# Attention in a two-block transformer kernel: transpose-mode turns, values as queries x channels, 64-row score products

## The chip, the cores and the metric

The kernel runs on one core of a Trainium2 chip. Its time is the device time of one execution in microseconds (us): the median of three runs. One more execution was taken by the hardware profiler, and everything read from the trace belongs to that one.

## The reference

Two layers of a latent transformer with context tokens and then one block of another design are computed in float32, on 512 latent tokens, 256 context tokens and a width of 1024. The change touches the three attentions alone. Cut to what matters:

```python
def dense_gqa_blocks(q, k, v):                # layer 0: 8 heads, 2 key heads, 768 keys
    s = jnp.einsum('bqkgd,btkd->bkgqt', qblk, k) * scale
    p = jax.nn.softmax(s, axis=-1).astype(v.dtype)
    return jnp.einsum('bkgqt,btkd->bqkgd', p, v)

def window_gqa_blocks(q, k, v, k_ctx, v_ctx, sink):   # layer 1: 16 heads, |q-k| <= 128, plus 256 context keys
    p = jax.nn.softmax(jnp.concatenate([s_w, s_c, s_s], axis=-1), axis=-1)   # s_s: one sink logit per head
    o = jnp.einsum('bkgqt,btkd->bqkgd', p[..., :BAND_LEN], vblk)
    o = o + jnp.einsum('bkgqt,btkd->bqkgd', p[..., BAND_LEN:BAND_LEN + C], v_ctx)

def chunked_attention(q, k, v, rel_bias):      # second block: 8 heads, chunks of 64, a relative bias
    scores = jnp.einsum('bnqhd,bnkhd->bhnqk', q, kb) * (ATT_HEAD_DIM ** -0.5) + bias
    p = jax.nn.softmax(jnp.where(valid, scores, min), axis=-1)
    out = jnp.einsum('bhnqk,bnkhd->bnqhd', p, vb)
```

In layer 0 the context queries attend to the context keys too.

## The kernel before

Channels lie on the partitions and tokens along the rows of a tile. Every large product is made in three passes of reduced float32: each operand is held as a high part and a low part, and high x high, high x low and low x high are summed in PSUM. Weight blocks of 128 x 1024 flow through a ring of four: SyncE loads them (`load_block`), ScalarE makes the high part (`split_hi`, L265), GpSimd the low part (`split_lo`, L271), TensorE uses them (`product`, L294). The engines run five programs written by hand; the order of the work is the order of the code, and semaphores hold them together.

The three attentions (`l0_att`, `l1_att`, `s_att`) use one set of functions, `att_pe`, `att_act`, `att_dve` and `att_pool`. The work is cut in units: one head and one tile of 128 queries. `ATT_ITERS` is 4, and one iteration has 12 units in l0, 16 in l1, 8 in s, so there are 48, 64 and 32 units. A unit has as many key blocks of 128 as its queries see: 6 in l0 (2 for context queries), 4 or 5 in l1, 1 to 4 in s; over all units that is 592 blocks. In l0 and l1 the two middle iterations are a loop on the engines (`Fori`), in s they are written out.

What TensorE does for a unit:

- `qk` (L1241): scores, queries x keys. A chunk of q holds two heads of 64 channels. GpSimd first copies the queries with the other head's 64 rows set to zero (`att_stage`, L1407), so that the product runs over 128 rows. In l1 the window mask is added by products with an identity (L1244), in s the relative bias.
- `turn` (L1258): for each block, `prob` (the exponentials, queries x keys) is the weight and `dg` the moving operand. `dg` is a diagonal with one over the row sum, so the product is the transposed and already divided probability, keys x queries, in ordinary float32.
- `values` (L1271): for each block three products, with v (128 keys x 64 channels) as the weight and the turned probabilities `pt_hi`, `pt_lo` (128 keys x 128 queries) moving. The result is 64 channels x 128 queries.

TensorE's order within unit u is `qk(u+2)`, `turn(u)`, `values(u-1)`. VectorE finds the row maximum (L1355, or L1358 and L1360 where there is a sink), makes the reciprocal and `dg` (L1377, L1379) and the low part `pt_lo` (L1366). ScalarE makes the exponentials with their row sum (L1301, and the sink's exponential, L1304), the high part `pt_hi` (L1331) and copies the result into `opair` (L1314), of which it makes the high part (L1319) and GpSimd the low part (L1426). `prob`, `pt_hi`, `pt_lo` and the score banks have two buffers each. In l0, VectorE also does twelve reductions over 128 x 1024 for the modulation vectors (`mod_block`, L339), six in the first iteration and six in the last.

## Time and profile before

| | us |
|---|---|
| median of 3 runs | 3029.43 |
| lowest, highest | 3028.75, 3034.0 |
| the profiled execution | 3029.36 |
| its span | 3027.6 |
| TensorE busy in it | 2899.5 |
| VectorE, ScalarE, GpSimd busy | 1686.7, 1050.2, 1145.4 |

The span is from the first instruction to the last; 1.8 us of the profiled execution's time lie around it. Busy is the union of an engine's instructions; since matmuls are pipelined and overlap in the record, the time from one start to the next is the price of one, and not its duration. A PE row with 128*128 has a weight of 128 rows x 128 columns; 128x64 or 128x512 after it is what moves through. An ordinary float32 product has two records for one instruction of the program.

### The profile page before, as it was taken

To read this page: it belongs to the slowest core of one execution; us is meant where nothing else is said; L and a number is where in the kernel's file an instruction comes from. 1 tells how busy PE (TensorE), PEld (TensorE's weight loads), DVE (VectorE), ACT (ScalarE), POOL (GpSimd) and SP (SyncE) were. 2 spreads that over 40 slices of the span, in tenths; PEclk is the share of its full clock that TensorE was granted. 3 is DMA by queue.
4 is the path that set the end of the run, shared out by engine and by line. 5 is a ranking of instruction groups with operands and counts; after the bars stand their busy time and mean duration, and the time that the engine had idled before them with its cause. 6 is when DMAs were issued, how large, how long until landed. Compare 5 with 4: busy or idle time off the path is not lost.

```text
span 3027.6 us, 43720 instructions
## 1 busy us (share of the span) xinstructions
PE 2899.5 (96%) x15898; PEld 2441.1 (81%) x15898; DVE 1686.7 (56%) x2794; ACT 1050.2 (35%) x1926; POOL 1145.4 (38%) x782
## 2 busy tenths in 40 slices
PE   8889999999999979999999999999999979899998
PEld 6779878888888769987888878888788758688886
DVE  5577886555545667775555564444544674432223
ACT  3247332111111437753222242222354673222222
POOL 1333223333333153323554544544353324334443
PEclk8989999999999999999999999999999999999999
DMA  5100333323232020032444423443202212122221
GB/s 217 53 28 8 120 111 135 115 89 113 88 119 90 28 78 2 1 118 92 146 169 171 145 91 139 145 152 132 101 26 81 81 61 99 68 84 97 97 97 56
DMA packets 78454, 290.91 MB, mean 96 GB/s; under 512 B 8833, under 2 KB 8961, under 8 KB 76929
## 3 DMA queue, kind: packets, MB, share of 16 engines
q1 hardware_dynamic: 78338, 289.36, 26.8%
q8 instruction: 73, 1.20, 0.2%
q14 instruction: 43, 0.35, 0.0%
HBM read 287.23 MB, written 2.10 MB: 96 GB/s over the span
## 4 chain that ended last, share of the span: by engine, by line
PE 85%; DVE 10%; ACT 3%; issue 1%; POOL 1%; DMA 0%; ACTq 0%; DVEq 0%; SPq 0%; POOLq 0%
PE ps L294 68%; PE ps L1258 4%; PE ps L1241 4%; PE ps L1271 3%; PE ps L494 2%; PE ps L350 1%; DVE ps L601 1%; PE ps L1516 1%; PE ps L1244 1%; DVE xl L608 1%; DVE rec L1711 1%; PE ps L955 1%; DVE r_g L1703 1%; DVE qn L1084 1%; PE ps L947 1%
## 5 line engine op out<-in xcount | busy, mean ns | idle before, releaser
L271 POOL TENSOR_TENSOR w_lo<-raw,w_hi 128x1024 fp32r<-128x1024 f32 x367 | 929.2, 2540 | 1445.4 <-ACT w_hi L265 1445.4
L265 ACT ACTIVATE w_hi<-raw 128x1024 fp32r<-128x1024 f32 x367 | 384.1, 1057 | 1355.0 <-PE ps L294 1251.1
L294 PE MATMUL ps<-n_hi,w_hi 128*128 128x512 f32 x1504 | 594.5, 395 | 12.4 <-DVE n_lo L1742 4.9
L294 PE MATMUL ps<-n_hi,w_lo 128*128 128x512 f32 x1504 | 587.4, 391 | 0.0
L294 PE MATMUL ps<-n_lo,w_hi 128*128 128x512 f32 x1504 | 587.4, 391 | 0.0
L820 DVE TENSOR_TENSOR y<-y,ps 128x512 f32<-128x512 f32 (+1 forms) x440 | 270.9, 633 | 266.1 <-PE ps L294 266.0
L339 DVE CUSTOM_DVE_ANT_0 dump<-modraw 128x1024 f32<-128x1024 f32 x212 | 356.9, 1683 | 13.8 <-DMA modraw<-mod_stream 7.9
L294 PEld LDWEIGHTS ps<-n_hi,w_hi 128*128 128x128 f32 x1504 | 283.7, 189 | 81.3 <-issue 11.7
L775 DVE TENSOR_TENSOR ps<-ffn_silu,ps 128x512 f32<-128x512 f32 x110 | 68.5, 641 | 481.0 <-PE ps L294 464.8
L294 PEld LDWEIGHTS ps<-n_lo,w_hi 128*128 128x128 f32 x1504 | 283.8, 189 | 60.6 <-issue 2.9
L294 PEld LDWEIGHTS ps<-n_hi,w_lo 128*128 128x128 f32 x1504 | 283.5, 189 | 59.3
L294 PE MATMUL ps<-h_hi,w_hi 128*128 128x512 f32 (+1 forms) x1072 | 291.8, 348 | 22.0 <-DVE h_lo L569 8.1
L294 PE MATMUL ps<-ffn_hi,w_hi 128*128 128x512 f32 x880 | 299.2, 372 | 1.3 <-DVE ffn_lo L782 0.8
L294 PE MATMUL ps<-ffn_lo,w_hi 128*128 128x512 f32 x880 | 297.7, 371 | 0.0
L294 PE MATMUL ps<-ffn_hi,w_lo 128*128 128x512 f32 x880 | 295.9, 369 | 0.0
L294 PE MATMUL ps<-h_lo,w_hi 128*128 128x512 f32 (+1 forms) x1072 | 293.4, 349 | 0.0
L294 PE MATMUL ps<-h_hi,w_lo 128*128 128x512 f32 (+1 forms) x1072 | 289.0, 345 | 0.0
L294 PEld LDWEIGHTS ps<-h_hi,w_hi 128*128 128x128 f32 x1072 | 169.7, 191 | 50.7 <-issue 20.3
L294 PEld LDWEIGHTS ps<-h_hi,w_lo 128*128 128x128 f32 x1072 | 171.1, 192 | 28.2
L294 PEld LDWEIGHTS ps<-h_lo,w_hi 128*128 128x128 f32 x1072 | 170.1, 192 | 24.3
L294 PEld LDWEIGHTS ps<-ffn_hi,w_hi 128*128 128x128 f32 x880 | 152.6, 188 | 33.3 <-DVE y L820 2.0
L294 PEld LDWEIGHTS ps<-ffn_hi,w_lo 128*128 128x128 f32 x880 | 153.6, 188 | 29.5
(292 smaller groups left out, 4287.1 us busy)
## 6 DMA issues: line engine op xcount, KB each, us to landing
raw<-w_stream SPq DMA_DIRECT2D x367, 512.0 KB, 3.4
modraw<-mod_stream SPq DMA_DIRECT2D x152, 512.0 KB, 3.2
mod_pair<-mod_first SPq DMA_DIRECT2D x7, 1024.0 KB, 12.5
xl<-x_in SPq DMA_DIRECT2D x1, 2048.0 KB, 7.6
out<-xl SPq DMA_DIRECT2D x8, 256.0 KB, 2.0
xc<-ctx_in SPq DMA_DIRECT2D x1, 1024.0 KB, 9.7
modraw<-mod_first SPq DMA_DIRECT2D x1, 1024.0 KB, 14.9
rel<-rel_in SPq DMA_DIRECT2D x1, 1024.0 KB, 4.7
```

What stands on the lines that cost most here:

```text
L265: nc.scalar.activation(w_hi[:, c % RING, :], raw[:, c % RING, :], ACT.Copy).then_inc(hi_ready, 1)
L271: nc.gpsimd.tensor_tensor(w_lo[:, c % RING, :], raw[:, c % RING, :], w_hi[:, c % RING, :].bitcast(F32), ALU.subtract).then_inc(lo_ready, 1)
L294: mm = nc.tensor.matmul(out, w[a], x[b][:, off:off + n], start=first and i == 0, stop=last and i == 2)
L339: nc.vector.tensor_tensor_reduce(where, modraw[:, slot, :], c_rows[:, m, :] if c < MOD2 else c2_row, 1.0, 0.0, ALU.mult, ALU.add, outs[m]) ...
L350: mm = nc.tensor.matmul(ps[:, 3, 2 * k:2 * k + 2], mod_pairs[k][:, 0, j * P:(j + 1) * P], c_cols[:, j, :], start=j == 0, stop=j == KC - 1)
L494: mm = nc.tensor.matmul(ps[:, sum_bank(name, si), 0:n], ones[:, :], square_buffer(name, k)[0][:, off:off + n], start=k == 0, stop=k == KC - 1)
L601: ins = nc.vector.scalar_tensor_tensor(out=product_chunk(name, k, si) if k in DVE_ADDS else t, in0=t, scalar=vec_g[:, slot, k, si:si + 1], ...
L775: nc.vector.tensor_tensor(up_bank(m % 2, si), f["silu"][:, m % 2, off:off + n], up_bank(m % 2, si), ALU.mult).then_inc(sem(f["name"] + "_h ...
L820: ins = nc.vector.tensor_tensor(acc, acc, out_bank(f, n, si, last), ALU.add)
L1241: mm = nc.tensor.matmul(score(u, col, w), (qs_hi, qs_lo)[x][:, qt % 2, half, :], a["k"][z][:, kc, kcol:kcol + w], start=i == 0, stop=i == ...
L1258: mm = nc.tensor.matmul(ps[:, 4 + g, (b - b0) * P:(b - b0 + 1) * P], prob[:, u % 2, b * P:(b + 1) * P], dg[:, u % 2, :], start=True, stop= ...
L1271: mm = nc.tensor.matmul(ps[0:HD, 6 + u % 2, 0:P], a["v"][z][:, x[4][b], a["vcol"](c, x)], (pt_hi, pt_lo)[p][:, u % 2, b * P:(b + 1) * P], ...
```

## The change

- `turn` becomes TensorE's transpose mode: the weight is `prob` as before, the moving operand is the identity. `dg` is gone.
- `values` swaps its operands: `pt_hi` and `pt_lo` (128 queries wide) are the weight and v (64 channels) moves. The result is 128 queries x 64 channels; ScalarE multiplies it by the reciprocal of the row sum while it copies it into `opair`.
- Since `opair` is now queries x channels, each pair of heads is turned once more (`pair_turn`), and the high and low parts of that are made by ScalarE and VectorE from PSUM.
- `qk` takes the 64 rows of the head straight from q and k. The staging on GpSimd is gone.
- In l1 the sink's logit is written as one more column of the scores, by an ordinary float32 product of `ones` with a 128 x 1 column. Row maximum, exponential and sum take it in; the separate steps for it are gone.
- The twelve modulation reductions in l0 go to GpSimd, which multiplies and then adds halves ten times (`mod_block_pool`).
- The loops over the iterations are written out on all engines.

```diff
-    opair, dg = at("opair", [2, P], SCR + 10240), at("dg", [2, P], SCR + 11264)
-    dump_att = at("dump_att", [BLK], SCR + 6144)
+    opair, mod_prod = at("opair", [2, P], SCR + 10240), at("mod_prod", [BLK], SCR + 6144)
...
+    def mod_block_pool(pool, c, outs):
+
+        ops, each = mods_of(c)
+        slot, turn = (c - MOD_FIRST) % MOD_RING, (c - MOD_FIRST) // MOD_RING
+        pool.wait_ge(mod_landed[slot], 16 * (turn + 1))
+        for m in range(each):
+            pool.wait_ge(mod_ops, ops + m)
+            nc.gpsimd.tensor_tensor(mod_prod[:], modraw[:, slot, :], c_rows[:, m, :], ALU.mult).then_inc(mod_halves, 1)
+            for j in range(HALVINGS):
+                pool.wait_ge(mod_halves, (ops + m - 2 * KC) * HALVINGS + j + 1)
+                n = BLK >> (j + 1)
+                last = j == HALVINGS - 1
+                nc.gpsimd.tensor_tensor(outs[m] if last else mod_prod[:, 0:n], mod_prod[:, 0:n], mod_prod[:, n:2 * n], ALU.add
+                                        ).then_inc(mod_ops if last else mod_halves, 1)
...
             for col, kcol, w in keys:
                 added = [m for m in more if col <= m[0] < col + w]
-                for i, (x, z) in enumerate(((0, 0), (0, 1), (1, 0))):
-                    mm = nc.tensor.matmul(score(u, col, w), (qs_hi, qs_lo)[x][:, qt % 2, half, :],
-                                          a["k"][z][:, kc, kcol:kcol + w], start=i == 0, stop=i == 2 and not added)
+                for j, (y, z) in enumerate(((0, 0), (0, 1), (1, 0))):
+                    mm = nc.tensor.matmul(score(i, col, w), a["q"][y][rows, qc, q0:q0 + P], a["k"][z][rows, kc, kcol:kcol + w],
+                                          start=j == 0, stop=j == 2 and not added)
...
+            if a["sink"]:
+                n = a["sink"](c, x)
+                mm = nc.tensor.matmul(score(i, score_width(a, i) - 1, 1), ones[:, :], sinks[:, n:n + 1], start=True, stop=True)
...
+        def pair_turn(p):
+            pe.wait_ge(a["s_o"], 2 * p + 2)
+            nc.tensor.transpose(PAIR_OUT, opair[:, p % 2, :], ident).then_inc(a["s_ot"], 1)
+
+        def turn(i):
+
+            pe.wait_ge(a["s_p"], i + 1)
+            for g, (b0, b1) in enumerate(a["groups"][i]):
+                if i > 0:
+                    pe.wait_ge(a["s_lo"], a["cum"][i - 1] + min(g + 1, len(a["groups"][i - 1])))
+                if g == 0 and pair_beside(i - 1) is not None:
+                    pe.wait_ge(a["s_m_lo"], pair_beside(i - 1) + 1)
+                if g == 0 and pair_beside(i) is not None:
+                    pair_turn(pair_beside(i))
                 for b in range(b0, b1):
-                    mm = nc.tensor.matmul(ps[:, 4 + g, (b - b0) * P:(b - b0 + 1) * P], prob[:, u % 2, b * P:(b + 1) * P],
-                                          dg[:, u % 2, :], start=True, stop=True)
+                    mm = nc.tensor.transpose(ps[:, 4 + g, (b - b0) * P:(b - b0 + 1) * P], prob[:, i % 2, b * P:(b + 1) * P], ident)
                 mm.then_inc(a["s_t"], 1)
...
                 for b in range(b0, b1):
-                    for i, (z, p) in enumerate(((0, 0), (0, 1), (1, 0))):
-                        mm = nc.tensor.matmul(ps[0:HD, 6 + u % 2, 0:P], a["v"][z][:, x[4][b], a["vcol"](c, x)],
-                                              (pt_hi, pt_lo)[p][:, u % 2, b * P:(b + 1) * P], start=b == 0 and i == 0,
-                                              stop=b == nb - 1 and i == 2)
+                    for j, (p, z) in enumerate(((0, 0), (0, 1), (1, 0))):
+                        mm = nc.tensor.matmul(head_out(i), (pt_hi, pt_lo)[p][:, i % 2, b * P:(b + 1) * P],
+                                              a["v"][z][:, blocks[b], a["vcol"](c, x)], start=b == 0 and j == 0,
+                                              stop=b == len(blocks) - 1 and j == 2)
             mm.then_inc(a["s_pv"], 1)
...
+        def out(i):
+
+            p, half = i // 2, i % 2
+            act.wait_ge(a["s_pv"], i + 1)
+            act.wait_ge(a["s_rinv"], i + 1)
+            if half == 0 and p >= 2:
+                act.wait_ge(a["s_ot"], p - 1)
+            nc.scalar.activation(opair[:, p % 2, half * HD:(half + 1) * HD], head_out(i), ACT.Copy,
+                                 scale=rinv[:, i % 4:i % 4 + 1]).then_inc(a["s_o"], 1)
+
+        def mixed_hi(p):
+            c, x = a["units"][2 * p]
+            act.wait_ge(a["s_ot"], p + 1)
+            nc.scalar.activation(a["out"][0][:, a["outchunk"](c, x), x[2]:x[2] + P], PAIR_OUT, ACT.Copy
+                                 ).then_inc(a["s_m_hi"], 1)
...
-        att_dve(dve, l0_att, att_mods)
+        att_dve(dve, l0_att)
...
-        att_pool_first(pool, l0_att, lambda eng: eng.wait_ge(l0_in["lo"], 5))
         split_lo(pool, FIRST["l0_pool"] + RING)
-        att_pool(pool, l0_att)
+        for c in range(MOD_FIRST, MOD_IN):
+            mod_block_pool(pool, c, [modv_a[m][:, c:c + 1] for m in range(2)])
```

The order of the instructions on TensorE in the fourth unit of l0, from its last score product on, before. In a row the moving operand stands first after the arrow and the weight second; `l_k` and `l_v` are keys and values, and the shape is that of the output.

```order
L1241 MATMUL ps<-l_k_hi,qs_lo 128x256
L1258 MATMUL ps<-dg,prob 128x128 [waits l0_att_lo,l0_att_diag]
L1258 MATMUL ps<-dg,prob 128x128 x2
L1258 MATMUL ps<-dg,prob 128x128 [waits l0_att_lo]
L1258 MATMUL ps<-dg,prob 128x128 x2
L1271 MATMUL ps<-pt_hi,l_v_hi 64x128 [waits l0_att_lo,l0_att_o]
L1271 MATMUL ps<-pt_lo,l_v_hi 64x128
L1271 MATMUL ps<-pt_hi,l_v_lo 64x128
```

The same place now; `loaded` is the tile that holds the identity.

```order
L1244 MATMUL ps<-l_k_hi,l_q_lo 128x256
L1255 MATMUL ps<-loaded,opair 128x128 [waits l0_att_o,l0_att_lo,l0_att_p]
L1268 MATMUL ps<-loaded,prob 128x128 x3
L1268 MATMUL ps<-loaded,prob 128x128 [waits l0_att_lo]
L1268 MATMUL ps<-loaded,prob 128x128 x2
L1280 MATMUL ps<-l_v_hi,pt_hi 128x64 [waits l0_att_lo,l0_att_o]
L1280 MATMUL ps<-l_v_lo,pt_hi 128x64
L1280 MATMUL ps<-l_v_hi,pt_lo 128x64
```

The number of instructions for a block stays at one turn and three value products. One turn for a pair of heads has come in, with its wait for ScalarE's copies, and `pt_hi` and `pt_lo` now stand second, as weights, where `l_v` stood.

On GpSimd, between the last weight split of l0's input stage and its first attention work, there stood the staging of queries:

```order
L271 TENSOR_TENSOR w_lo<-raw,w_hi 128x1024 [waits hi_ready] x3
L1407 TENSOR_TENSOR qs_hi<-l_q_hi,loaded 128x128 [waits lo_ready,l0_in_lo]
L1407 TENSOR_TENSOR qs_hi<-l_q_hi,loaded 128x128
L1407 TENSOR_TENSOR qs_lo<-l_q_lo,loaded 128x128 x2
L1407 TENSOR_TENSOR qs_hi<-l_q_hi,loaded 128x128 x2
L1407 TENSOR_TENSOR qs_lo<-l_q_lo,loaded 128x128 x2
```

In its place stand the modulation reductions, twelve times a product and ten halvings:

```order
L270 TENSOR_TENSOR w_lo<-raw,w_hi 128x1024 [waits hi_ready] x4
L349 TENSOR_TENSOR mod_prod<-modraw 128x1024 [waits mod_ops,mod_landed0]
L354 TENSOR_TENSOR mod_prod<-mod_prod 128x512 [waits mod_halves]
L354 TENSOR_TENSOR mod_prod<-mod_prod 128x256 [waits mod_halves]
L354 TENSOR_TENSOR mod_prod<-mod_prod 128x128 [waits mod_halves]
L354 TENSOR_TENSOR mod_prod<-mod_prod 128x64 [waits mod_halves]
L354 TENSOR_TENSOR mod_prod<-mod_prod 128x32 [waits mod_halves]
```

What TensorE's first score product waited for on GpSimd is no longer there; GpSimd reads instead what SyncE loads into `modraw`.

## Rows read from the trace of the kernel before

**Rows 1.** The page: its first line, the engines' busy time, TensorE's clock.
```profile
PE 2899.5 (96%) x15898; PEld 2441.1 (81%) x15898; DVE 1686.7 (56%) x2794; ACT 1050.2 (35%) x1926; POOL 1145.4 (38%) x782
...
PEclk8989999999999999999999999999999999999999
```

**Rows 2.** Busy time by stretch, middle of each attention: stretch, length, engines, PEclk, DMA.
```profile
204.00:330.00 126.00, 121.82 (x1258) 116.86 (x1256) 101.60 (x242) 85.36 (x240) 41.91 (x102) 1.00 0.06 22
...
1150.00:1322.00 172.00, 172.00 (x1862) 171.91 (x1861) 136.16 (x415) 123.04 (x387) 53.93 (x142) 1.00 0.01 1
...
2250.00:2296.00 46.00, 45.15 (x417) 42.99 (x414) 33.14 (x108) 33.63 (x124) 18.41 (x48) 1.00 0.01 2
```

**Rows 3.** L1271 alone in the whole of each attention: PE, PEld, PEclk, DMA.
```profile
190.00:334.00 144.00, 52.30 (x672) 46.83 (x672) 0.97 0.07 23
1136.00:1327.00 191.00, 67.33 (x864) 59.95 (x864) 0.99 0.01 1
2227.00:2296.00 69.00, 22.06 (x240) 18.41 (x240) 0.98 0.00 1
```

**Rows 4.** Groups by line and shape, TensorE: count, busy us, mean ns, idle before.
```profile
L1258 PE MATMUL ps<-dg,prob 128*128 128x128 f32 x1184 | 160.7, 279 | 5.0 <-DVE pt_lo L1366 4.8
```

**Rows 5.** Timeline of one six-block unit in l0, TensorE: start, us, engine, line.
```profile
241.03 0.45 PE L1241 MATMUL ps<-l_k_hi,qs_hi 128*128 128x512 f32 x1
...
242.13 1.50 PE L1258 MATMUL ps<-dg,prob 128*128 128x128 f32 x12
243.38 0.30 PE L1271 MATMUL ps<-pt_hi,l_v_hi 128*64 128x128 f32 x1
243.53 0.22 PE L1271 MATMUL ps<-pt_lo,l_v_hi 128*64 128x128 f32 x1
243.58 0.22 PE L1271 MATMUL ps<-pt_hi,l_v_lo 128*64 128x128 f32 x1
...
244.54 0.45 PE L1241 MATMUL ps<-l_k_hi,qs_hi 128*128 128x512 f32 x1
```

**Rows 6.** Timeline, first and last of 34 products in l0's input stage.
```profile
87.79 0.28 PE L947 MATMUL ps<-w_hi,h_lo 128*128 128x128 f32 x1
...
91.47 0.27 PE L947 MATMUL ps<-w_hi,h_lo 128*128 128x128 f32 x1
```

**Rows 7.** Timeline of the first modulation products, two moving columns each.
```profile
26.96 1.95 PE L350 MATMUL ps<-c_cols,mod_pair 128*128 128x2 f32 x16 [1.08 <-DVE n_rstd L539]
28.77 1.93 PE L350 MATMUL ps<-c_cols,modraw 128*128 128x2 f32 x16
30.55 19.79 PE L350 MATMUL ps<-c_cols,mod_pair 128*128 128x2 f32 x94
```

**Rows 8.** Busy time by stretch, as rows 2, around those products and around L947.
```profile
20.00:30.00 10.00, 8.92 (x47) 5.94 (x45) 5.38 (x8) 6.60 (x11) 1.70 (x1) 1.00 1.02 424
30.00:40.00 10.00, 10.00 (x54) 10.00 (x53) 9.61 (x11) 0.00 (x0) 3.94 (x2) 0.55 1.01 413
40.00:50.00 10.00, 10.00 (x49) 10.00 (x49) 8.71 (x16) 0.00 (x0) 0.00 (x0) 0.50 0.04 16
80.00:90.00 10.00, 10.00 (x92) 10.00 (x91) 4.91 (x4) 1.46 (x3) 4.12 (x2) 1.00 0.17 54
```

**Rows 9.** TensorE's waits in l0's attention: us in total, times, longest.
```profile
PE ps L1258 <- DVE pt_lo L1366: 4.4, 6, 2.1
```

**Rows 10.** Timeline of the start of l1's attention.
```profile
1131.81 0.22 DVE L2006 CAST ident_r<-loaded 128x128 fp32r<-128x128 f32 x1
...
1136.11 0.83 DVE L1086 TENSOR_TENSOR l_q_lo<-qraw,l_q_hi 128x512 fp32r<-128x512 f32 x1 [0.70 <-ACT l_q_hi L983]
...
1136.53 0.55 PE L1241 MATMUL ps<-l_k_hi,qs_hi 128*128 128x256 f32 x1 [16.57 <-POOL qs_lo L1407]
...
1138.37 0.69 DVE L1358 TENSOR_REDUCE smax<-ps 128x1 f32<-128x512 f32 x1 [1.44 <-PE ps L1244]
```

**Rows 11.** Timeline, GpSimd beside l0's attention and l1's input stage.
```profile
191.56 2.38 POOL L271 TENSOR_TENSOR w_lo<-raw,w_hi 128x1024 fp32r<-128x1024 f32 x1 [11.98 <-ACT w_hi L265]
...
243.57 0.76 POOL L1407 TENSOR_TENSOR qs_lo<-l_q_lo,loaded 128x128 fp32r<-128x128 f32 x2
...
1118.77 1.79 POOL L1126 TENSOR_TENSOR tsh<-tsh,loaded 128x512 f32<-128x512 f32 x1 [2.81 <-DVE tsh L1080]
```

More of the change, by code:

```diff
@@ L81 @@
           ("edges", [4, 2, 8]),
-          ("nsink", [16]),
+          ("sinks", [16]),
           ("relc", [8]),
@@ L1176, in pool_dve, with attention @@
             ins.then_inc(st["mix_lo"], 1)
-    def attention(name, units, q, k, v, out, qchunk, kchunk, vcol, outchunk, next_block, extra=None, sink=None,
-                  unroll=False):
+    def attention(name, units, q, k, v, out, qchunk, kchunk, vcol, outchunk, next_block, ready, extra=None, sink=None):
+        whole = [(c, x) for c in range(ATT_ITERS) for x in units]
         groups = []
-        for x in units:
+        for _, x in whole:
             nb = len(x[4])
@@ L1193, in attention @@
             cum.append(cum[-1] + len(g))
-        return dict(name=name, units=units, q=q, k=k, v=v, out=out, qchunk=qchunk, kchunk=kchunk,
-                    vcol=vcol, outchunk=outchunk, extra=extra, sink=sink, groups=groups, cum=cum, nu=len(units), next=next_block, unroll=unroll, d_steps=3 if sink else 2,
+        return dict(name=name, units=whole, q=q, k=k, v=v, out=out, qchunk=qchunk, kchunk=kchunk, vcol=vcol,
+                    outchunk=outchunk, ready=ready, extra=extra, sink=sink, groups=groups, cum=cum, n=len(whole), next=next_block,
@@ new lines, in score_width, with turned, head_out, pair_beside @@
+    def score_width(a, i):
+        return P * len(a["units"][i][1][4]) + (1 if a["sink"] else 0)
+    def turned(g, b0, b1):
+        return ps[:, 4 + g, 0:(b1 - b0) * P]
+    def head_out(i):
+        return ps[:, 6 + i % 2, 0:HD]
+    PAIR_OUT = ps[:, 4, 3 * P:4 * P]
+    def pair_beside(i):
+        return (i - 3) // 2 if i >= 3 and i % 2 else None
+    def att_pe(pe, a, free):
+        def qk(i):
+            c, x = a["units"][i]
+            _, half, q0, keys, _, _ = x
+            a["ready"](pe, c, x)
+            rows = slice(half * HD, (half + 1) * HD)
+            qc, kc = a["qchunk"](c, x), a["kchunk"](c, x)
+            more = a["extra"](c, x) if a["extra"] else []
@@ L1274, in values @@
             mm.then_inc(a["s_pv"], 1)
-        def body(c, first, last):
-            for u in range(nu):
-                n = ahead(a, c, u, last)
-                if n:
-                    qk_next(c, u, n)
-                turn(c, u, first)
-                n = behind(a, c, u, first, 1, nu)
-                if n:
-                    values(*n, first)
-            if last:
-                values(c, nu - 1, False)
-        free(pe)
-        qk(0, 0)
-        qk(0, 1)
-        att_loop(pe, a, body)
@@ L1411, in att_pool_first @@
-    def att_pool_first(pool, a, ready):
-        ready(pool)
-        pool.wait_ge(lo_ready, a["next"] + (RING - 1 - a["next"]) % RING + 1)
-        for qt in range(2):
-            att_stage(pool, a, 0, qt, True)
-    def att_pool(pool, a):
-        nt = a["nu"] // 2
-        def m_lo(c, p):
-            pool.wait_ge(a["s_m_hi"], c * nt + p + 1)
-            x = a["units"][2 * p]
+        free(pe)
+        qk(0)
+        qk(1)
+        for i in range(a["n"]):
+            if i + 2 < a["n"]:
+                pe.wait_ge(a["s_p"], i + 1)
+                qk(i + 2)
+            turn(i)
+            if i >= 1:
+                values(i - 1)
@@ L1425, in m_lo @@
             n = a["outchunk"](c, x)
[L1426 removed]
+            dve.wait_ge(a["s_m_hi"], p + 1)
+            nc.vector.tensor_tensor(a["out"][1][:, n, x[2]:x[2] + P], PAIR_OUT,
                                     a["out"][0][:, n, x[2]:x[2] + P].bitcast(F32), ALU.subtract).then_inc(a["s_m_lo"], 1)
[L1429 to L1438 removed]
@@ L1440, in att_pool @@
-        att_loop(pool, a, body)
+        row_max(0)
+        row_max(1)
+        inverse(0)
+        for i in range(a["n"]):
+            if i + 1 < a["n"]:
+                inverse(i + 1)
+            if i + 2 < a["n"]:
+                row_max(i + 2)
+            for g in range(len(a["groups"][i])):
+                low(i, g)
+                if g == 0 and pair_beside(i) is not None:
+                    mixed_lo(pair_beside(i))
+        mixed_lo(a["n"] // 2 - 1)
     def m_done(eng, a):
-        eng.wait_ge(a["s_m_lo"], ATT_ITERS * a["nu"] // 2)
+        eng.wait_ge(a["s_m_lo"], a["n"] // 2)
```

247 lines of the change are left out of this document (66 added, 181 removed).

## The prediction

> **What bounds the kernel now.** I read the page first, then the busy time by stretch, then the timeline of one unit. TensorE is busy for 96% of the span, at nearly full clock [rows 1]. In the middle of the attentions it is busy for 121.8 of 126, 172.0 of 172 and 45.2 of 46 us, while VectorE has at most 81% and ScalarE at most 73% [rows 2]. So what the change does to TensorE's stream counts one for one, and what it takes off the other engines counts only where TensorE waited for them: in l0 4.4 us for `pt_lo` [rows 9] and one wait of 16.6 us at the head of l1's attention [rows 10]. The attentions take 144, 191 and 69 us with their edges [rows 3], 404 of the span. That is the field of the change.
>
> The timeline of a six-block unit of l0 gives the prices [rows 5]. It repeats after 244.54 - 241.03 = 3.51 us: scores 1.10 (241.03 to 242.13), turns 1.25 for 12 records (0.104 each, so 0.208 a block), values 1.16 for 18 products. Within the values, the first step of a unit is 0.15 and the others 0.06: 243.53 to 243.58 and on to the next.
>
> **Values.** 672 + 864 + 240 = 1776 products [rows 3]. Their weight had 64 columns and 128 moved; now the weight has 128 columns and 64 move. What does such a product cost? The nearest row is L947: the same kind of number, weight of 128 columns, 128 moving. It goes at (91.47 - 87.79) / 33 = 0.112 us [rows 6], nearly twice the 0.060 of the values, though as many columns move: the difference is the weight's width. And L350, where only two columns move, still takes 1.81 / 16 = 0.113 [rows 7]. So with a weight of 128 columns the load sets the pace, whether 2 or 128 columns move, and 64 lies between them. I take 0.112. The change is 1776 x 0.052 = +92.4 us. From below, 0.030 would be half of 0.060, if only moving columns counted: 1776 x -0.030 = -53 us. I keep that end for a rival.
>
> **Turns.** 1184 records in two for each of 592 blocks [rows 4]. The weight keeps 128 columns. If transpose mode takes one pass, the floor from rows 6 and 7 is 0.112 a block against 0.208: 592 x -0.096 = -56.8 us. If it stays at two records of 0.104, the gain is nothing. I take one pass, since an identity times data needs no product of parts, and keep 0 as the other end.
>
> **Turns of pairs and sinks.** Half the units make a pair turn: (48 + 64 + 32) / 2 = 72 x 0.112 = +8.1. The sink is one ordinary float32 product per unit of l1, two records, each with a weight of 128 columns and one column moving, as L350 has two: 64 x 2 x 0.112 = +14.3.
>
> **Score products of 64 rows.** The number of products and of moving columns stays, so I cost them as before where the load of the next weight is still hidden behind the running product. There is no row with 64 of 128 rows in this trace. What is new is that 64-row and 128-row products alternate: in l0 and s twice and in l1 two to four times a unit, 48 x 2 + 64 x 3 + 32 x 2 = 352 changes. The nearest row is the change from `turn` to `values`, whose first step is 0.15 and not 0.06, so about 0.08 more [rows 5]. 352 x 0.08 = 28 us at most, 0 at least; I take the middle, +14. The upper bound of another kind, that no weight load is hidden in them, is priced below.
>
> **The Trainium skill against these rows.** The Trainium skill, "TensorE: Matmul & The Clock Gate", section "Back-to-back issue gap", gives about 81 ns for each pair of weight load and product at 128 moving columns, which would mean that a load of 128 columns is partly hidden. By that figure, as an estimate, values would cost +37 us, turns -75, pair turns and sinks +16, and with the other terms the sum would be about -10 us, the other sign. The 33 steps at 0.112 here do not agree with it, and here the measurement decides.
>
> **Waits.** In l1 the 16.6 us look like a gift, and are not. The first score product now waits only for the mask and identity, ready at 1132.0, so it can start 4.5 us earlier. But the next in line is VectorE: it is busy with the last chunk of q until 1136.9 and starts its row maximum at 1138.4 [rows 10]. Nothing behind it moves by more than 1.5 us: -1.5. In l0 the modulation work leaves VectorE, and the `pt_lo` waits of 4.4 us go, since VectorE was idle for a fifth of that stretch even with that work in it [rows 2]: -4.4. Against this, each attention now ends with copy, pair turn, high part and low part, one step more than before: about 0.7 us three times, +2. In units of one and two blocks TensorE's share of a unit is short, and the longer chain turn, pair's high part, `pt_hi`, `pt_lo`, next turn may show: +2. Behind the new waits for `s_o` and `s_m_lo` TensorE's whole stream is queued, and in a unit of four blocks or more about 2 us of value products stand between them and their source, which hides them. Together -2.
>
> GpSimd's twelve reductions: 2.4 us for the product of 128 x 1024, at most 1.8 for 512, 0.4 at 128 (two in 0.76) [rows 11], so about 0.9 for 256, and six smaller ones at no more than 0.38. That is at most 7.8 each and 94 in all, from about 194 us on, done at about 288 where the next weight split is due after 334. They are hidden. If they weren't, the weight stream of l0's output stage would wait.
>
> **The sum.** 92.4 - 56.8 + 8.1 + 14.3 + 14 - 2 = +70 us. The profiled execution took 3029.36, 0.07 below the median of the runs, so the same number serves for both: 3029.4 + 70 = 3099 us. With 0 to 28 for the changes of height and a few us either way for the waits, this case has a range of its own of 3080 to 3120.
>
> **Rivals.**
> A. The clock falls. During L350 TensorE has a product in flight all the time, and the granted clock still goes from 1.00 to 0.55 and 0.50, that is from 2.4 to 1.2 GHz, soon after those products with two moving columns began; each then takes 0.21 (19.79 / 94) [rows 7, 8]. In the changed unit far fewer columns move: 3 x 768 for the scores, 768 for the turns, 18 x 64 for the values, 4224, where 7680 moved before in a similar time. Against it: at L947, with 128 columns moving in 0.112 us, the clock stayed at 1.00 [rows 8], and 4224 columns in about 3.9 us are the same share. The new attention has about 404 + 70 = 474 us. At the low level for a quarter of it, the cost is 118 more, 3218; for all of it, 3570. It decides from some 20 us of low clock. 13%, of which 10 beyond my range.
> The Trainium skill, the same page, section "Part 4: PE-mode transpose", says that transposes in this mode do not count as TensorE activity for the full clock. No row here shows it; it speaks for this rival and would take 768 of the 4224 columns away.
> B. The load of the weight doesn't bind in the values, and columns moved set the price. Then values cost nothing more at 0.060, and the sum is 70 - 92 = -22: 3007 us. At 0.030 it would be 2954. Anything between 0.030 and 0.072 is this rival. Rows 6 and 7 speak against it, at two different widths. It decides as soon as a value product costs less than 0.072 (70 / 1776 below 0.112). The Trainium skill's 81 ns of the section above, "Back-to-back issue gap" of "TensorE: Matmul & The Clock Gate", with the turns at that price too, would end at 3020, on this side; its chance is counted here. 7%, all faster.
> C. In 64-row products the next weight isn't loaded beside the running product. 240 + 480 + 96 = 816 score products (three for each run of keys in 144 units) would pay up to 0.112 more: +91, 3190 us. For it: the trace has no such product. Against it: 128-row ones hide the load fully. 9%.
> D. Transpose mode does not do what its name says here, and a turn costs its 0.208: +57, 3156 us. 10%.
> E. The terms cancel to within 6 us of before. 3%.
> The forecast has 58%.
>
> **How the numbers follow.** What a measurement of this kernel can tell from no change is about 0.2%, 6 us. Faster is B, 7%; the same is E, 3%; slower is the rest, 90%. The range reaches from 3070, ten below the own range since some price may lie between the bounds, to 3195, so that C and D are in it. Left out are B, E and most of A, 20%.
>
> **What would show it.** Right: in the changed profile the value products start 0.11 us apart, the turns have 592 + 72 records 0.11 apart, a six-block unit of l0 takes 3.8 to 4.0 us, TensorE is still without gaps in the middle of the attentions, the first score product of l1 starts near 1132 plus what l0 has lost and the turns behind it hardly earlier than before. Wrong: value products 0.06 or less apart (B), score products with gaps of 0.1 between them (C), 1184 turn records (D), a clock of 0.5 inside an attention (A), or GpSimd late with l0's output weights.

## The result and the profile after

The changed kernel takes **3492.1 us** (median of four runs, 3481.0 to 3493.9) against 3029.1 for the kernel before beside it: ratio 1.152, 95% interval 1.149 to 1.155. The forecast was 3099, with a range up to 3195. Rival A, the falling clock, is what happened, over the whole of the three attentions.

The first lines of the page after, which answer to [rows 1]:

```profile
span 3479.2 us, 41669 instructions
...
PE 3357.9 (97%) x15506; PEld 2845.1 (82%) x15506; DVE 1630.7 (47%) x2569; ACT 1033.9 (30%) x1862; POOL 1084.8 (31%) x554
...
PEclk8955579999999975555699999999995699999999
```

TensorE is as busy as before, so the busy shares alone say nothing. The clock row does: three valleys of 5, at the three attentions. The record of the granted clock holds 982 us at the lower level (1.2 GHz), where the kernel before has 128. Three stretches make up 887 of them, one over each attention: 290.1 us, 454.0 and 143.4. The attentions themselves, from the first score product to the end of the last pair turn, take 284.4, 440.9 and 140.4 us, and 862 us of them are at the lower level.

Busy time by stretch of the kernel after (columns as in [rows 2]), inside l0's and l1's attention and around the start of s's:

```profile
250.00:450.00 200.00, 200.00 (x814) 183.03 (x815) 64.64 (x153) 64.47 (x186) 26.64 (x49) 0.50 0.03 9
1300.00:1700.00 400.00, 399.50 (x1738) 376.39 (x1737) 107.94 (x266) 109.56 (x325) 0.00 (x0) 0.50 0.00 1
2605.00:2610.00 5.00, 2.50 (x14) 1.65 (x12) 2.62 (x6) 4.18 (x6) 2.36 (x1) 0.84 0.00 0
2610.00:2620.00 10.00, 9.37 (x28) 6.99 (x28) 3.56 (x14) 3.90 (x17) 0.00 (x0) 0.50 0.00 1
```

TensorE has no gap of note in the first two stretches and still has half of its clock. VectorE and ScalarE are idle for two thirds of the time or more, and TensorE's waits for them do not show there. In s the clock falls within microseconds of the attention's start and stays down.

The timeline of TensorE in l0, answering to [rows 5]: the end of the scores, the turns, the value products of a two-block unit, and the next scores. Columns: start, us, engine, line.

```profile
266.21 0.41 PE L1244 MATMUL ps<-l_k_hi,l_q_lo 64*128 64x256 f32 x1
266.56 1.54 PE L1268 MATMUL ps<-loaded,prob 128*128 128x128 f32 x6
267.75 0.40 PE L1280 MATMUL ps<-l_v_hi,pt_hi 128*128 128x64 f32 x1
267.96 0.40 PE L1280 MATMUL ps<-l_v_lo,pt_hi 128*128 128x64 f32 x1
...
268.81 0.40 PE L1280 MATMUL ps<-l_v_hi,pt_lo 128*128 128x64 f32 x1
269.14 0.79 PE L1244 MATMUL ps<-l_k_hi,l_q_hi 64*128 64x512 f32 x1
269.74 0.62 PE L1244 MATMUL ps<-l_k_lo,l_q_hi 64*128 64x512 f32 x1
270.17 0.62 PE L1244 MATMUL ps<-l_k_hi,l_q_lo 64*128 64x512 f32 x1
```

Value products start 0.21 apart, six turns take 267.75 - 266.56 = 1.19 us, 0.20 each, and a 512-wide score step is 270.17 - 269.74 = 0.43 and not 0.235. Everything runs at about half speed. The seam, as I call the change between 128-row and 64-row products, is seen too: from the last value product to the first 64-row product it is 269.14 - 268.81 = 0.33 and not 0.21.

The turns by themselves, answering to [rows 4] (duration min/median/max, first and last start):

```profile
L1268 PE MATMUL ps<-loaded,prob x592: 417/421/474, 197.0 to 2739.7; 128*128 128x128 f32 x198
```

One record a block: transpose mode takes one pass, as forecast.

**How much is the clock?** From one level to the other a value product goes from 0.213 to 0.111 us (the latter at full clock, in an experiment below), a 512-wide score step from 0.43 to 0.235: 48 and 45% less. Whole units of this very stream were seen at both levels in a5_warm_entry below: the same seven units of s took 31.20 and 16.95 us, 46% less. On the 982 - 128 = 854 us of additional low clock that makes 390 us, an estimate from these seven units; a second reckoning, further below, leaves 345. The span grew by 3479.2 - 3027.6 = 452, so the clock is by far the greater part.

### The profile page after: what moved, and what is told of

It reads as the page before. It is cut to its first block, busy times and chain, and to the rows that moved or that the text cites. A ratio compares the mean times of both kernels' runs of the same rounds, so it can differ in the third digit from the quotient of the medians.

```text
span 3479.2 us, 41669 instructions
## 1 busy us (share of the span) xinstructions
PE 3357.9 (97%) x15506; PEld 2845.1 (82%) x15506; DVE 1630.7 (47%) x2569; ACT 1033.9 (30%) x1862; POOL 1084.8 (31%) x554
## 3 DMA queue, kind: packets, MB, share of 16 engines
q8 instruction: 76, 1.25, 0.1%
## 4 chain that ended last, share of the span: by engine, by line
PE 88%; DVE 8%; ACT 2%; issue 1%; POOL 1%; DMA 0%; SPq 0%; ACTq 0%; DVEq 0%; POOLq 0%
PE ps L293 59%; PE ps L1280 10%; PE ps L1244 7%; PE ps L1268 4%; PE ps L1247 2%; PE ps L509 2%; PE ps L1255 1%; PE ps L365 1%; DVE ps L616 1%; PE ps L1454 1%; PE ps L1250 1%; DVE xl L623 1%; DVE rec L1649 1%; PE ps L970 0%; DVE r_g L1641 0%
## 5 line engine op out<-in xcount | busy, mean ns | idle before, releaser
L1345 DVE TENSOR_REDUCE negm<-ps 128x1 f32<-128x768 f32 (+6 forms) x144 | 101.5, 706 | 481.5 <-PE ps L1250 261.1
L1280 PE MATMUL ps<-l_v_hi,pt_hi 128*128 128x64 f32 x512 | 205.4, 401 | 0.0
L1280 PE MATMUL ps<-l_v_hi,pt_lo 128*128 128x64 f32 x512 | 205.3, 401 | 0.0
L1280 PE MATMUL ps<-l_v_lo,pt_hi 128*128 128x64 f32 x512 | 205.3, 401 | 0.0
```

Source lines behind the costliest of these rows:

```text
L1280: mm = nc.tensor.matmul(head_out(i), (pt_hi, pt_lo)[p][:, i % 2, b * P:(b + 1) * P], a["v"][z][:, blocks[b], a["vcol"](c, x)], start=b == ...
L1345: nc.vector.reduce_max(negm[:, i % 4:i % 4 + 1], score(i, 0, score_width(a, i)), AX.X, negate=True).then_inc(a["s_negm"], 1)
```

## Experiments

Fourteen kernels. "Low" is the time at the lower clock in the profiled execution, summed over the record of the granted clock. The kernel before had 128, the changed one 982. The ratio is to runs of the kernel before in the same job.

| run | built on | us | ratio (95%) | low |
|---|---|---|---|---|
| a1_turn_plain | after | 3451.6 | 1.142 (1.130 to 1.154) | 720 |
| a2_v_weight | after | 3051.7 | 1.009 (1.005 to 1.014) | 201 |
| a3_rows128 | after | 3076.8 | 1.018 (1.012 to 1.023) | 150 |
| a4_wide_values | after | 3496.1 | 1.157 (1.150 to 1.163) | 969 |
| a5_warm_entry | after | 3507.4 | 1.157 (1.152 to 1.162) | 921 |
| b1_pt_weight | before | 3102.4 | 1.023 (1.018 to 1.029) | 140 |
| b2_transpose | before | 2992.2 | 0.987 (0.980 to 0.994) | 135 |
| b3_rows64 | before | 3100.4 | 1.023 (1.020 to 1.026) | 170 |
| c1_weight_rows | before | 3365.2 | 1.114 (1.109 to 1.120) | 640 |
| e1_half_rows128 | after | 3318.5 | 1.099 (1.089 to 1.108) | 580 |
| e2_one_extra | after | 3555.4 | 1.177 (1.174 to 1.180) | 1053 |
| f1_one_short | after | 3184.5 | 1.053 (1.049 to 1.057) | 328 |
| d1_turn_scaled | before | 3030.7 | 1.004 (1.002 to 1.005) | 149 |
| d2_scaled_pool | before | 2988.4 | 0.987 (0.984 to 0.991) | 136 |

### One part taken back from the changed kernel

**a1_turn_plain**: turns as ordinary products.

```
- nc.tensor.transpose(ps[...], prob[...], ident)
+ nc.tensor.matmul(ps[...], prob[...], ident, start=True, stop=True)
```

> The changed kernel with the 592 turns of probabilities as ordinary float32 products with the identity again (two records each), all else as changed. Theory T2 (transpose-mode products do not count for the clock, and that is what holds it low): the granted clock in the attentions goes back to 1.0 and the time falls to about 3492 - 433 + 57 = 3115 us. Theory T1 (too few columns move, and the value products are most of it): the turns now move four times the columns, so the clock may come back in part; if it stays low, the turns cost 592 x 0.2 us more at the low clock, 3600. Theories T3 (64-row products count for half) and T4 (the clock falls at the entrance and can't come back): stays low, 3600.

Low clock falls from 982 to 720 us only. The transposes have a share in it and are not the cause alone.

**a2_v_weight**: v as the weight again, 128 columns moving.

```
- matmul(head_out(i), pt[...], v[...])
+ matmul(ps[0:HD, 6 + i % 2, 0:P], v[...], pt[...])
```

> The changed kernel with v as the weight and pt moving again in the value products (64 channels x 128 queries in PSUM, read as before by 128 x 64, so that the output is not the reference's; the copies, turns and waits stay). T1: the clock comes back, and the products cost 0.060 again: 3492 - 433 - 92 = about 2970 us. T2, T3, T4: the clock stays low; a value product then takes 0.107 in place of 0.213, about 3300 us.

The clock is back: low 201, and of the 73 us more than before most is in the first units of l1's and s's attention.

**a3_rows128**: score products over all rows, everything else as changed.

```
- rows = slice(half * HD, (half + 1) * HD)
+ rows = slice(0, P)
```

> The changed kernel with score products over all 128 rows of q and k (both heads are summed, so the output is not the reference's). T3: the clock comes back, about 3060 us; also the changes of height are gone, at most 28 us less. T1, T2, T4: the clock stays low, 3450 to 3490 us.

The clock is back here as well, and with it the prices at full clock can be read. Timeline of TensorE in this kernel:

```profile
257.97 0.82 PE L1268 MATMUL ps<-loaded,prob 128*128 128x128 f32 x6
258.55 0.28 PE L1280 MATMUL ps<-l_v_hi,pt_hi 128*128 128x64 f32 x1
258.66 0.28 PE L1280 MATMUL ps<-l_v_lo,pt_hi 128*128 128x64 f32 x1
...
261.21 0.30 PE L1255 MATMUL ps<-loaded,opair 128*128 128x128 f32 x1
261.35 0.82 PE L1268 MATMUL ps<-loaded,prob 128*128 128x128 f32 x6
```

Value products are 0.11 apart, as priced. Six turns take 0.58 (0.097 each), a little under the price of 0.112, and a pair turn 0.14, a little over it. This is the changed kernel without changes of height and almost without the low clock, and it is 3076.8 - 3023.3 = +54 us against before in its job; my terms for the same parts were 92 - 57 + 8 + 14 - 2 = +56.

**a4_wide_values**: the value products move 128 columns of v where 64 are wanted, and only those are read.

```
- matmul(head_out(i), pt[...], v[..., vcol])
+ matmul(ps[:, 6 + i % 2, 0:P], pt[...], v[..., both heads' columns])
```

> The changed kernel with 128 columns of v moving in each value product (both heads of the pair, of which the right 64 are read), so the output is the same; only the columns moved go up by 1776 x 64. If the load of the weight sets the pace, it costs nothing at either clock. T1: the clock comes back at least for a large part: 3060 us if all of it. T2, T3, T4: no change, 3490 us.

Twice the columns in the values change neither the time nor the clock, and the clock row is that of the changed kernel, digit for digit. A six-block unit moves 5376 columns here, and has the low clock; in a3 it moves the 4224 of the changed kernel, and has the full one. So my own argument for rival A, too few columns moved, does not name the cause. The run says one more thing: with a weight of 128 columns, moving 128 costs no more than moving 64, here at the low clock.

**a5_warm_entry**: 60 dense products once in each attention, behind the third unit's scores, in case the clock is lost at the entrance and merely not regained.

```
+ if i == 0:
+     for _ in range(60): nc.tensor.matmul(ps[:, 7, 3 * P:4 * P], ones, ones, start=True, stop=True)
```

> The changed kernel with 60 ordinary float32 products of 128 x 128 by 128 columns put between the third unit's score products and the first turn of each attention, in a bank that nothing uses yet. They take 13 us at the full clock and up to 26 at the low one, three times, and after them the clock is at 1.0. T4 (the clock falls in the gap at the entrance and only cannot come back): it stays at 1.0 through the attentions, about 3492 - 433 + 60 = 3120 us. T3 (64-row products count for less, so the stream of the changed unit doesn't hold the full clock whatever came before): it falls again soon after the 60 products, 3530 to 3560 us.

Busy time by stretch of this kernel, around those products in l0, and then over the same seven units of s's attention in its first and in its second iteration:

```profile
197.00:220.00 23.00, 23.00 (x170) 22.16 (x169) 5.01 (x9) 4.17 (x10) 20.22 (x35) 0.87 0.09 25
220.00:235.00 15.00, 15.00 (x64) 13.82 (x62) 4.62 (x10) 4.50 (x12) 13.13 (x24) 0.50 0.11 35
235.00:300.00 65.00, 65.00 (x270) 59.74 (x268) 21.42 (x52) 21.98 (x65) 39.65 (x73) 0.50 0.11 33
...
2662.70:2679.65 16.95, 16.95 (x116) 14.45 (x115) 9.63 (x33) 10.24 (x40) 0.00 (x0) 1.00 0.01 2
2682.21:2713.41 31.20, 31.20 (x116) 26.48 (x115) 9.75 (x33) 10.36 (x40) 0.00 (x0) 0.50 0.00 1
```

The clock rises with the dense products and falls again behind them, though TensorE has no gap: it is the attention's steady stream that loses it. In s the full clock outlasts them by seven units, and so this run has the changed stream at both levels: 16.95 and 31.20 us for the same 116 products.

### One part alone on the kernel before

**b1_pt_weight** (values' operands exchanged):

```
- matmul(ps[0:HD, 6 + u % 2, 0:P], v[...], pt[...])
+ matmul(ps[:, 6 + u % 2, 0:HD], pt[...], v[...])
```

> The kernel before with the value products' operands swapped alone: pt_hi, pt_lo as the weight, 64 columns of v moving (the copy that follows reads another layout, so the output is not the reference's). By the price of the load, 1776 x 0.052 = 92 us more, 3115 us, at a full clock, if the fall needs 64-row score products as well (T3). If narrow value products are enough for it (T1), low clock in the attentions and 3400 us or more.

+71 us at full clock. The step is 0.111, as priced. But in the kernel before the first value step of a unit, where the weight's width had just changed, was 0.15 [rows 5]; now it is 0.11 like the others:

```profile
245.78 1.50 PE L1258 MATMUL ps<-dg,prob 128*128 128x128 f32 x12
247.04 0.28 PE L1271 MATMUL ps<-l_v_hi,pt_hi 128*128 128x64 f32 x1
247.15 0.28 PE L1271 MATMUL ps<-l_v_hi,pt_lo 128*128 128x64 f32 x1
```

144 units save 0.09 each, 13 us, and the 4.4 us of waits of [rows 9] go too: 92.4 - 13 - 4.4 = 75. The sum had not let go of that step. The two runs of this kernel are 13 us apart, so 71 and 75 do not differ.

**b2_transpose** (transpose mode, the division left out):

```
- matmul(ps[...], prob[...], dg[:, u % 2, :], start=True, stop=True)
+ transpose(ps[...], prob[...], ident)
```

> The kernel before with the turns in transpose mode with the identity alone (the division is left out, so the output is not the reference's; its steps on VectorE stay). T3: full clock, 592 x 0.1 = 57 us less, 2966 us. T2 (transposes do not count for the clock): the clock falls at least in part, and the time is over 3100 us.

-39 us at full clock. Six turns take 0.58 here too, 0.67 less than the 1.25 before; over 592 blocks that is 66 us, more than the 57 of the sum. Part of what is missing is a new wait. TensorE's waits in this kernel (us in total, times, longest), answering to [rows 9]:

```profile
PE ps L1258 <- DVE pt_lo L1366: 19.9, 48, 2.4
```

A six-block unit now takes 2.85 us of TensorE, and VectorE can't always follow: this wait is 15 us more than the 5 of the kernel before. The other 12 us that are missing of the 66 are not placed, and the two runs here are 16 us apart.

**b3_rows64** (scores over the head's 64 rows):

```
- matmul(score, qs[:, ...], k[:, ...])
+ matmul(score, qs[half * HD:(half + 1) * HD, ...], k[half * HD:(half + 1) * HD, ...])
```

> The kernel before with score products over the 64 rows of the head alone, from the staged copy (the output stays the same). If changes of height cost 0.08 each: 28 us more, 3052 us; if they cost nothing, 3024. T3 in its strong form (64-row products alone let the clock fall): low clock in part, over 3100 us. T3 in its weak form (they count for less, but turns and value products as before make up for it): full clock.

+69 us, though low clock is only 42 us more. The rest is the seams. First the second product of a unit in the kernel before, behind the one at 241.03 of [rows 5]; then timelines of TensorE and of its weight loads (PEld) in this kernel:

```profile
241.31 0.40 PE L1241 MATMUL ps<-l_k_lo,qs_hi 128*128 128x512 f32 x1
```

```profile
244.84 0.50 PE L1241 MATMUL ps<-l_k_hi,qs_hi 64*128 64x512 f32 x1
245.18 0.39 PE L1241 MATMUL ps<-l_k_lo,qs_hi 64*128 64x512 f32 x1
245.42 0.39 PE L1241 MATMUL ps<-l_k_hi,qs_lo 64*128 64x512 f32 x1
...
248.56 0.22 PE L1272 MATMUL ps<-pt_hi,l_v_lo 128*64 128x128 f32 x1
248.71 0.50 PE L1241 MATMUL ps<-l_k_hi,qs_hi 64*128 64x512 f32 x1
```

```profile
248.71 0.18 PEld L1241 LDWEIGHTS ps<-l_k_hi,qs_hi 64*128 64x128 f32 x1
248.81 0.19 PEld L1241 LDWEIGHTS ps<-l_k_lo,qs_hi 64*128 64x128 f32 x1
249.05 0.18 PEld L1241 LDWEIGHTS ps<-l_k_hi,qs_lo 64*128 64x128 f32 x1
```

Entering the 64-row products costs 0.15 and not 0.06 from the last value product (248.56 to 248.71), and the first 512-wide step is 0.34 where it was 241.31 - 241.03 = 0.28: the weight at 248.71 is loaded at its product's start, whereas the next ones are loaded well ahead of theirs (248.81 for the product at 249.05). A whole six-block unit takes 248.71 - 244.84 = 3.87 against 3.51 [rows 5], for two changes: 0.18 each. That unit is on the dear side: taken step by step, wherever both kernels had the full clock, b3's attentions take 47.5 us more over 316 changes, 0.15 each. Over 352 changes that is 53 us, and the rest of the 69 goes with the additional low clock. Within the 64-row products nothing is lost, 0.24 per 512 columns as before: rival C does not occur.

None of the three parts loses the clock alone.

### Pairs and doses

**c1_weight_rows**: b1 and b3 together on the kernel before.

> The kernel before with two parts of the change: the value products' operands exchanged (the sums of one unit are then read in the wrong layout, so the output isn't the reference's) and score products over the head's 64 rows. Turns stay ordinary products of two records with the division in them. The two parts alone cost +79 and +69 us and kept the clock. If it takes these two together to lose the clock, as the version with ordinary turns suggests (3452, low clock for 720 us): low clock for 400 us or more, 3350 to 3500 us. If all three parts are needed, or the division at the output: the clock stays near 0.97 and the costs add, 3023 + 79 + 69 = 3170 us.

3365: low clock 640 us. Values with pt as the weight and 64-row scores lose it together, without transposes and with the division where it was. The other two pairs stand in a2 (transposes and 64-row scores, low 201) and a3 (transposes and values, low 150), each with the smaller parts of the change, and they keep it. Page of this kernel, clock row, and l1's attention by stretch:

```profile
PEclk8967999999999965655799999999998998999999
```

```profile
1220.00:1640.00 420.00, 420.00 (x1977) 396.98 (x1975) 154.64 (x436) 134.87 (x408) 56.68 (x147) 0.56 0.00 1
```

In l0 and s the row stays at 6 or above, where the changed kernel has 5. The rest of the change, transposes, pair turns, sinks and division, adds 982 - 640 = 342 us of low clock to these two; a1 puts 262 of that kind on the transposes.

**e1_half_rows128**: scores over 128 rows in every second unit.

```
+ rows = slice(0, P) if i % 2 else slice(half * HD, (half + 1) * HD)
```

> The changed kernel with the score products of every second unit over all 128 rows (both heads' rows, so these scores are wrong; the output isn't the reference's). With all units at 128 rows it took 3077 us at full clock, with none 3492. If the rows in use decide and there is a point from which the clock holds: near 3100 (half of the changes of height left) with low clock under 200 us. If the loss goes with the share of 64-row products: low clock for some 400 to 550 us and about 3280.

3318 with low clock 580: a little above the expectation of a share. There is no single point from which the clock holds; it goes up and down. The three attentions do not share the loss alike. Low clock of each attention's length, in us, wherever the clock is lost in part:

| run | l0 | l1 | s |
|---|---|---|---|
| a1_turn_plain | 127 of 240 | 449 of 480 | 24 of 99 |
| c1_weight_rows | 110 of 229 | 383 of 431 | 24 of 95 |
| e1_half_rows128 | 74 of 184 | 371 of 398 | 20 of 85 |
| f1_one_short (below) | 31 of 175 | 146 of 303 | 16 of 88 |

Each time l1 loses most. What sets it apart, its score products of at most 256 columns, its masks or its up to four changes of height a unit, was not tested.

**e2_one_extra**: one more 128-row product in each unit, ahead of its scores.

```
+ matmul(score(i, col, w), q[0][:, qc, ...], k[0][:, kc, kcol:kcol + w], start=True, stop=True)
```

> The changed kernel with one more product over 128 rows (one pass, up to 512 columns moving, its result overwritten by the first score product) ahead of the score products of each of the 144 units. Its own cost is 144 x about 0.15 to 0.21, 20 to 30 us at full clock. If the low clock comes from too little of what 128-row products with many columns do, this brings it back: 3110 to 3200. If it is the load-bound stretch of values and turns itself, or the changes of height, the clock stays low and it takes 3520 us.

3555, low 1053: the clock does not come back at all. One more 128-row product a unit beside the 64-row products does not help.

**f1_one_short**: scores over 128 rows, and ahead of them one 64-row product of 128 columns in each unit.

```
+ matmul(score(i, col, P), q[0][short, qc, ...], k[0][short, kc, kcol:kcol + P], start=True, stop=True)
- rows = slice(half * HD, (half + 1) * HD)
+ rows, short = slice(0, P), slice(half * HD, (half + 1) * HD)
```

> The changed kernel with score products over all 128 rows (both heads' rows, so the scores and the output aren't the reference's) and, ahead of them in each of the 144 units, one product over 64 rows with 128 columns moving, whose result is overwritten. That leaves 288 changes of height, against 352 in the changed kernel, and takes nearly all 64-row work away. Without the short products it took 3077 at full clock. If changes of height let the clock fall: low clock for 500 us or more, over 3350 us. If it is the work of the 64-row products itself: full clock, 3077 + 144 x (0.3 to 0.5) = 3120 to 3150 us.

3184, low 328, between the two expectations. Its clock row:

```profile
PEclk8889899999999975899999999999999998999999
```

l0 and s keep nearly the full clock; l1 is low for its first 138 us and then, with the same sequence of units, nearly all the time full:

```profile
1155.00:1290.00 135.00, 131.61 (x593) 127.46 (x594) 41.15 (x92) 38.24 (x108) 4.10 (x2) 0.50 0.00 1
1300.00:1440.00 140.00, 140.00 (x1176) 135.75 (x1174) 69.91 (x173) 69.01 (x213) 0.00 (x0) 1.00 0.01 1
```

So with 288 changes of height and one short 64-row product a unit, 178 of the 832 us of low clock that separate a3 from the changed kernel are there. That the rest belongs to the work of the 64-row products is likely and not shown: this stream holds either level for over 100 us, so such shares need not add up.

### Versions that might beat both

**d1_turn_scaled**: kernel before, transposes, and the probabilities multiplied by `rinv` ahead of the turn; first group of blocks on VectorE in place of `dg`, second on GpSimd.

```
- nc.vector.tensor_scalar(dg[:, u % 2, :], ident, rinv[...], None, ALU.mult)
+ nc.vector.tensor_scalar(prob[:, u % 2, 0:w], prob[:, u % 2, 0:w], rinv[...], None, ALU.mult)
+ nc.gpsimd.tensor_tensor(prob[second group], prob[second group], rinv[...].to_broadcast(...), ALU.mult)
```

> The kernel before with turns in transpose mode and the division done on the probabilities ahead of the turn, half of the columns on VectorE in place of the diagonal, half on GpSimd. Scores stay at 128 rows and values keep v as the weight. Same output. The version with the division left out took 2992 us. VectorE's step keeps about its 0.30 us, GpSimd gets some 0.9 us more per unit beside its 0.84 for q, under the 2.84 of a unit. If both hide: 2990 to 3000, faster than both kernels. If VectorE, which TensorE already waits for there, gets longer by 0.1 to 0.2 per unit: 3000 to 3020. If GpSimd is late with its half: over 3030.

3030.7, ratio 1.004, slightly slower than before. VectorE's busy time and mean in 70 us of l0, and TensorE's wait for it:

```profile
L1382 DVE TENSOR_SCALAR prob<-prob,rinv 128x384 f32<-128x384 f32 (+1 forms) x27 | 13.5, 498 | 0.9
```

```profile
PE ps L1260 <- DVE pt_lo L1368: 49.6, 69, 2.6
```

The step costs 0.50 and not 0.30, and TensorE waits 49.6 us for VectorE: the cause of the second outcome, with the time of the third.

**d2_scaled_pool**: the whole scaling on GpSimd, nothing on VectorE.

```
- nc.vector.tensor_scalar(dg[:, u % 2, :], ident, rinv[...], None, ALU.mult)
+ nc.gpsimd.tensor_tensor(prob[:, u % 2, 0:w], prob[:, u % 2, 0:w], rinv[...].to_broadcast([P, w]), ALU.mult)
```

> As the kernel before with transposes and scaled probabilities, but the whole scaling on GpSimd and no diagonal or scaling on VectorE. Same output. GpSimd's steps took 0.67 us for 384 columns, so about 1.35 a unit beside 0.84 for q, under the 2.84 of a unit; VectorE has 0.30 a unit less to do than in the version without a division (2992). If VectorE was what TensorE waited for: 2975 to 2990 us, faster than both kernels. If GpSimd is now late, or slows VectorE beside it: 3000 to 3040.

**2988.4 us**, ratio 0.987 (0.984 to 0.991), 1.3% faster than before, with nothing of the computation left out. GpSimd's group in 70 us of l0, and TensorE's wait:

```profile
L1423 POOL TENSOR_TENSOR prob<-prob,rinv 128x768 f32<-128x768 f32 (+1 forms) x26 | 29.7, 1141 | 4.8 <-DVE rinv L1377 4.8
```

```profile
PE ps L1258 <- POOL prob L1423: 22.2, 40, 2.5
```

The wait for `pt_lo` is down to 2.4 us and one for GpSimd has come, 22.2 us. Of the three parts taken alone, the transposes are the one that pays.

## Why the prediction was wrong

The step that failed is the clock, which the sum put at nothing. Rival A named the right event and the right place, and had 13%. What the runs showed in its place: 862 us of the attentions at the low clock, worth 345 to 390 of the 452 us by the two reckonings below. A's upper price, 3570, doubled the whole time of the attentions; the units seen at both levels grow by a factor of 1.84.

- **The argument against A** was that 4224 columns in 3.9 us are the same share as at L947, where the clock held [rows 6, 8]. It took columns moved as what counts. a4 moved twice as many in the values and changed nothing; a3 moved the same columns over more rows and had the full clock. Columns moved were not the measure, so the comparison with L947 proved nothing. Neither the 64-row products nor transpose mode had a row in the trace, and I had priced both as time alone.
- **The argument for A** was counted in columns too. The Trainium skill's hint, "TensorE: Matmul & The Clock Gate", section "Part 4: PE-mode transpose" (a transpose in this mode does not count as busy in the same way), is borne out only in part here. Transposes alone keep the clock (b2, low 135 against 128), and without them the changed kernel still has 720 us of low clock (a1). They have a part in it, 262 us of low clock, and are not its whole cause.
- **Values +92**: the product's price was right (0.111), the term 13 too high, because the first step's 0.15 goes with the change of width; b1 measured +71, with the 4.4 us of waits in it. Rival B does not occur, and neither do the 81 ns of the Trainium skill, "TensorE: Matmul & The Clock Gate", section "Back-to-back issue gap".
- **Turns -57**: one record, 0.097 each, which makes -66. b2's -39 is this less a new wait for VectorE of some 15 us and 12 us not placed. In the changed kernel that wait is not there. Rival D does not occur.
- **Changes of height +14, at most 28**: b3 measured +69, some 53 of it in the seams, 0.15 each. I took the step from `turn` to `values`, a change of the weight's width, as the nearest row. It is another thing: at a change of height the next weight is not loaded ahead. The upper bound of this term was too low by a factor of two.
- **Pair turns and sinks +22, waits -2**: not measured alone. a3, all but the changes of height, came to +54 where the terms give +56. That is luck in part: the values' term was 13 too high, the turns' 9 too small a gain, and some 10 of the 54 are a3's own 22 us of additional low clock.
- **GpSimd's reductions** end at 280.4 us (288 foretold) and are hidden. **l1's start** has its wait for `ident_r` of 12.4 us in place of 16.6, as argued.

Without the fall of the clock the parts would have made +54 (a3) plus about 53 for the seams: 3029 + 107 = 3136 us, inside the range. Against the span that leaves 452 - 107 = 345 for the clock, where seven units at both levels give 390. Some 10 of the 45 between them are the low clock within a3's 54, and 8 are a stretch outside: from the end of l0's attention to the start of l1's it is 802.9 us before, 795.9 in a3 and 787.5 in the changed kernel. The rest is not placed; a seam of 0.12, as a5's seven units have over a3's (16.95 against 15.24 us, 14 changes), would take away 10 more.

**What stays open** is what the chip counts. The runs exclude columns moved by the values (a4), transposes alone (b2), either of the other two parts alone (b1, b3), the entrance (a5), and the lack of one more 128-row product a unit (e2). They show that 64-row scores with value products whose weight has 128 columns are enough (c1), that each of the two is necessary in the changed kernel (a2, a3), that the loss is graded, with half of the 64-row scores (e1) or with one short 64-row product a unit (f1), and falls on l1 first. The product of rows and columns in use does not order them either: in a six-block unit a3 adds 64 rows to 2304 columns of the scores and a4 adds 64 columns of 128 rows to 18 value products, 147456 both, and only a3 brings the clock back. Whether it is the height itself, the work of 64-row products or the changes between the heights is not shown.

## What to carry to other kernels

When a change alters the form of TensorE's products (rows, width of the weight, transpose mode), compare each form with what the trace has seen at full clock; a form without a row, in a stretch of hundreds of microseconds, is not covered by a comparison in columns moved, and its price at the low clock can be larger than all other terms together. Look at the clock row of the page before any explanation by instructions: a TensorE that is 97% busy at 0.50 is not a bound that its instruction count explains. And take a bundle of changes apart: here one of the three parts taken alone paid (2988 us, with its division on GpSimd), and the bundle hid it.

## What the hardware showed that I had not expected

- Three parts that keep the clock one by one (low clock 140, 135 and 170 us) lose it together: 982 us; two of them, 640.
- Between 128-row and 64-row products the next weight is not loaded ahead: 0.15 us for each change at full clock as a mean (b3: 47.5 us over 316 changes; 3.87 against 3.51 for a unit with two).
- The same sequence of units ran at either level for over 100 us: in f1's l1 at 0.50 from 1155 to 1290 us and at 1.00 from 1300 to 1440.
- With a weight of 128 columns, 64 or 128 moving columns cost the same: at full clock 0.111 us (a3, b1) and 0.112 [rows 6]; at the low one a4 and the changed kernel differ by 4 us in 3492.
- VectorE's scaling in SBUF of 384 columns and fewer took 0.50 us as a mean, with GpSimd scaling beside it, where the 128-column diagonal took 0.30, and GpSimd's for 768 columns 1.14 us as a mean with the shorter ones.
